# A fused four-layer kernel: evictions of first halves put ahead of weight conversions, three conversions put sooner, and the log-sum transposes put between two gate halves

## The reference

```python
q, k = rope(rms(aq)), rope(rms(ak))
ya = sliding_window_sink_attention(q, k, v, sink) * silu(ag)
qk = silu(causal_depthwise_conv(concat([mq, mk]), conv_w, conv_b))
hm = rms_norm(mlstm_chunkwise(*split(qk), mv, log_i, log_f))
ym = hm * sigmoid(mo) * silu(mgate)
x = x + concat([ya, ym]) @ w_out
```

## Time and the profile before

| what | value |
|---|---|
| median of 3 runs | 3051.35 us (3050.33 to 3055.56) |
| profiled execution: its own time | 3051.55 us |
| profiled execution: span in the trace | 3049.7 us |
| mean granted TensorE clock | 0.987 |
| PE busy | 2944.1 us, 97% |
| DVE, ACT, POOL busy | 53%, 41%, 6% |
| DMA | 250.24 MB, 82 GB/s on average |

### The profile page before, as it was taken

One profiled execution on the slowest core, in us unless ns is written; L12 is line 12 of the kernel. 1 busy time (PEld: TensorE's weight loads), 2 busy tenths in 40 slices (PEclk: granted clock), 3 DMA queues, 4 the chain that ended last, 5 costly groups with the idle time before them and its releaser, 6 DMA issues.

```text
span 3049.7 us, 44919 instructions
## 1 busy us (share of the span) xinstructions
PE 2944.1 (97%) x18366; PEld 2568.1 (84%) x18366; DVE 1629.9 (53%) x3259; ACT 1262.7 (41%) x2640; POOL 187.1 (6%) x207
## 2 busy tenths in 40 slices
PE   8999999999999999999999999999999999999998
PEld 7898888988888899898888877887888888877886
DVE  6767545367674453677433554325677433554334
ACT  5555423255553233566324433223566323433222
POOL 2100000020000000100000000000100000000000
PEclk9999999999999999999999999999999999999999
DMA  3111322211113222322232222233322232222322
GB/s 115 51 51 52 106 68 63 87 56 51 59 51 106 68 88 82 117 72 79 85 116 85 75 77 76 90 97 97 114 84 79 76 119 89 77 76 77 96 97 76
DMA packets 99735, 250.24 MB, mean 82 GB/s; under 512 B 8597, under 2 KB 44845, under 8 KB 99274
## 3 DMA queue, kind: packets, MB, share of 16 engines
q1 hardware_dynamic: 99530, 247.37, 25.8%
HBM read 239.60 MB, written 6.50 MB: 81 GB/s over the span
## 4 chain that ended last, share of the span: by engine, by line
PE 80%; DVE 11%; ACT 5%; issue 2%; POOL 1%; DMA 1%; DVEq 0%; SPq 0%; POOLq 0%; ACTq 0%
PE ps L92 77%; PE ps L95 3%; ACT Z L98 2%; DVE Z L109 2%; DVE Z L101 2%; DVE ZR L101 1%; DVE cl L101 1%; ACT ch L98 1%; DVE Z L105 1%; DVE stat L122 1%; DVE Z L119 1%; DMA st<-in_stream_dram 1%; POOL stat L101 1%; DVE stat L109 1%; ACT sq L98 1%
## 5 line engine op out<-in xcount | busy, mean ns | idle before, releaser
L101 DVE TENSOR_TENSOR cl<-st,ch 128x1024 fp32r<-128x1024 f32 (+1 forms) x436 | 500.4, 1156 | 635.2 <-ACT ch L98 634.8
L92 PE MATMUL ps<-hl,ch 128*128 128x264 f32 (+1 forms) x2816 | 835.7, 340 | 0.0
L92 PE MATMUL ps<-hh,ch 128*128 128x512 f32 (+1 forms) x2624 | 806.3, 347 | 26.6 <-ACT Z L98 12.3
L92 PE MATMUL ps<-hh,cl 128*128 128x512 f32 (+1 forms) x2624 | 795.3, 343 | 0.0
L98 ACT ACTIVATE ch<-st 128x1024 fp32r<-128x1024 f32 (+1 forms) x436 | 428.9, 990 | 513.5 <-PE ps L92 428.1
L92 PEld LDWEIGHTS ps<-hh,ch 128*128 128x128 f32 x2624 | 455.1, 191 | 98.1 <-ACT Z L98 18.4
L92 PEld LDWEIGHTS ps<-hl,ch 128*128 128x128 f32 x2816 | 487.2, 190 | 59.5
L92 PEld LDWEIGHTS ps<-hh,cl 128*128 128x128 f32 x2624 | 456.2, 190 | 59.2
L92 PE MATMUL ps<-ZR,ch 128*128 128x264 f32 (+2 forms) x1856 | 445.9, 337 | 5.5 <-DVE cl L101 5.1
L98 ACT ACTIVATE Z<-ps 64x128 f32<-64x128 f32 (+7 forms) x506 | 217.3, 437 | 432.1 <-PE ps L92 318.5
L92 PEld LDWEIGHTS ps<-ZR,ch 128*128 128x128 f32 x1856 | 305.3, 190 | 48.9 <-issue 12.8
(11 more groups left out here) (133 smaller groups left out, 3211.1 us busy)
## 6 DMA issues: line engine op xcount, KB each, us to landing
st<-in_stream_dram SPq DMA_DIRECT2D x372, 512.0 KB, 3.5
st<-in_stream_dram SPq DMA_DIRECT2D x64, 256.0 KB, 3.3
Z<-decay_rows SPq DMA_DIRECT2D x8, 904.0 KB, 6.1
Z<-bias_lines SPq DMA_DIRECT2D x16, 448.0 KB, 3.8
ya_spill<-Z SPq DMA_DIRECT2D x8, 512.0 KB, 4.6
Z<-ya_spill SPq DMA_DIRECT2D x2, 2048.0 KB, 7.5
Z<-in_x_dram SPq DMA_DIRECT2D x4, 512.0 KB, 5.3
Z<-in_mem_dram SPq DMA_DIRECT2D x2, 1024.0 KB, 5.7
```

Source lines behind the costliest of these rows:

```text
L92: return Ins(self, self.e and self.e.matmul(o, a, b, start=start, stop=stop, skip_group_check=True))
L101: return Ins(self, self.e and self.e.tensor_tensor(o, a, b, op))
```

## The change

It moves steps in the list, and adds or removes none.

1. `proj` of a first half no longer puts its conversion at once. The conversion is owed, and `put` places it right behind the next step whose name ends in `ev`. This concerns every first half that goes through `proj`, some 90 of them; `projr`, `mvmm`, `kvk`, `dvmm`, `lvmm` and the units with one half are as before.
2. In `mem_kv` the conversion that followed `kvk` 3 stands ahead of it ("one memory piece").
3. In `block1` the conversion that followed the first `o1` stands ahead of ys 6 to 13 ("one output piece").
4. In `block2` the first half of `lg(0)` stands between `mq(1)` and `lse2`, and its second half ahead of group 1's `pn`, where both stood.

```diff
+        self.owed = False
 
     def put(self, *step):
         self.o.append(step)
+        if self.owed and step[0].endswith("ev"):
+            self.owed = False
+            self.weights()
...
     def proj(self, key, nid, T, u, h, last=None):
         last = h == 1 if last is None else last
         self.put("proj", key, nid, T, u, h, last)
-        for _ in range(2 if last and not h else 1):
-            self.weights()
+        if last:
+            for _ in range(1 if h else 2):
+                self.weights()
+        else:
+            self.owed = True
...
         def step(c):
             if c < 4:
+                if c == 3:
+                    self.weights()
                 self.put("kvk", l, c, self.take(2, l, "kv", c))
-                self.weights()
+                if c < 3:
+                    self.weights()
                 return
...
+        self.weights()
         for k in range(6, 14):
             put("ys", l, k)
...
             if n != 1:
                 put("o1", l, n, p, 0, 8)
-                self.weights()
+                if n:
+                    self.weights()
...
-        def lg(c):
-            u = self.unit(2, l, 8704 + 256 * c)
-            for h in range(2):
+        def lg(c, hs=(0, 1)):
+            if 0 in hs:
+                st["lg"] = self.unit(2, l, 8704 + 256 * c)
+            u = st["lg"]
+            for h in hs:
                 self.proj(("lg", l, 2 * c + h), nid, 512, u, h)
                 put("lgev", l, 2 * c + h, self.nsq(), self.ngr())
         put("lse0", l)
         mq(0)
         put("lse1", l)
         mq(1)
+        lg(0, (0,))
         put("lse2", l)
         for g in range(3):
             if g == 1:
-                lg(0)
+                lg(0, (1,))
```

## The result

The changed kernel takes 3078.6 us, the median of 4 runs (3077.29 to 3078.76), beside 3050.84 us for the kernel before in the same session (3047.77 to 3055.56). The ratio is 1.0092, 95% interval 1.008 to 1.0104: slower by 0.9%. The forecast had the sign and the places right and the size too small: +17.3 against about +27.8, and the range ended at 3076.

What follows compares the result with a forecast made beforehand. TensorE, busy 2944.1 of 3049.7 us (97%), was taken as the bound. Terms -9.1 -1.2 +15.0 +6.6 +4 +2 = +17.3, added to 3051.55, gave 3068.8 us; range 3057 to 3076.

Steps and rivals of the forecast that it cites:

- lse: Block 2's log-sum part: edits 1 and 4 make pn end 7.5 us later, which reaches PE; +15.0 for two layers.
- the single gap of over 5 us: Sign of being right: a new PE gap of 5 us or more ahead of eT 2, which waits for pn.
- fB, +6.6 of gap: Block 2's fB 0 and fB 1: DVE's copies start 1.46 and 1.84 us later; +6.6 for both layers.
- Clock, +4 at fB and +2 at eT: Half clock after new PE gaps: 1.0 us each at four fB gaps and, for each layer, at eT.
- My case of half clock at all six gaps in full: Rival: 1.7 us at each new gap (+4.2) and lse at 9, about 3076 us; chance 0.15.
- Block 1, -9.1 and -1.2 for the gate: Block 1: gaps -5.7 and clock -3.4 from edits 1 and 3; attention gate's half-clock stretch, both layers, -1.2.
- the query halves: Block 1: eviction first lets PE start earlier; -0.95 and -0.96 at step 3, -1.2 at halves 5 and 7, -1.7 clock.
- mA 0: Block 1: a conversion comes beside another one on DVE; +0.8 us (0.3 to 1.3) in the first layer.
- The price of one stretch, 1.7: A half-clock stretch of 3.4 us costs about 1.7 us where PE is dense.
- Edit 2, 0: Memory piece: its cl waits for its copy either way, 0; without the cover of ACT's norms, 1.2 us per layer.
- little change: Rival: lse costs 3.8 a layer, no new half clock at fB or eT; +3.9, 3055.5 us; chance 0.10.
- faster: Rival: lateness at lse and fB does not reach PE; block 1's -10.3 is left, 3041.2 us; chance 0.04.

Runs made afterwards that it cites:

- experiment 4: The changed kernel, but first halves mg 2 and gt(0,0), ahead of fB 0 and fB 1, convert before their eviction as before: 3064.54 us, 1.0046.
- experiment 8: The changed kernel with 12 unused identity products added in PE's gaps at fB 0 and fB 1 of each block 2 layer: 3069.62 us, 1.006.
- experiment 1: The changed kernel with eviction-first kept for block 1's halves only, edit 4 undone, edits 2 and 3 kept: 3043.16 us, 0.9972.
- experiment 3: The changed kernel with edit 4 undone, lg(0) whole again ahead of group 1's pn: 3061.34 us, 1.0033.
- experiment 9: The kernel of experiment 1 without eviction-first for attention gate 6, and with yasp 5 to 7 moved behind fB 2: 3042.35 us, 0.9971.
- experiment 10: The kernel of experiment 1 without eviction-first for attention gate 6: 3044.41 us, 0.998.
- experiment 2: The kernel before with edit 4 alone, the first half of lg(0) ahead of lse2: 3062.6 us, 1.0039.

## Why the prediction was wrong: the price of the lower clock, and edit 1 in block 1

**lse, +15.0 of lateness.** Right: the gap of 5.3, `pn` starting 10 us and ending 7.3 us late, and that all of it reaches PE (7.4). In the second layer it is 8.6, 1.3 of them because `lg(0)` ran at 0.50 for twice as long. Which row waits first was not right, nor the single gap of over 5 us: I had `eT` 2; it was `eT` 1, for group 0's products, and 1.51, 1.21 and 0.19.

**fB, +6.6 of gap.** Right to 0.05 us at both places.

**Clock, +4 at fB and +2 at eT.** This is the step that failed. At fB it is 7.5 to 9.0 (experiments 4 and 8), behind `eT` 2.0 and 2.5, and 1.3 in the second layer's `lg(0)`: together some 13.5 to 15 for the 6 that I took. Three things are in it. I took 1.0 of 1.7 as a mean for each gap at fB, and both gaps of 2.7 in both layers brought a stretch, worth 1.6 to 1.7 each in the rows; the one behind fB 2 also grew from 3.4 to 6.8 in the first layer. Behind `eT` I priced one stretch of 3.4 us, at most 1.7, and the clock stayed at 0.50 for 10 us, with waits of 1.51, 1.21 and 0.19 (in the second layer 1.42, 1.28 and 0.77) ahead of it and in it. And I had no term for a longer stretch in `lg(0)`. My case of half clock at all six gaps in full was still 1.7 for each, so the range's upper end rested on the same prices.

**Trainium skill, "TensorE: Matmul & The Clock Gate", section "Why this matters for your kernels".** The Trainium skill says there that only idle gaps longer than those at fB bring the clock down, so by it the four stretches would have stayed away. The runs decide against it: in the traces with gaps of 2.71 at fB, 11 of 12 such gaps are followed by 0.50, and with matmuls in them, in experiment 8, the time falls by 9.0 us.

**Block 1, -9.1 and -1.2 for the gate.** Edit 3 was right (-5.2 measured, -4.6 forecast). Edit 1 was forecast at -2.8 net in gaps there and up to -2.9 in clock, and is worth nothing that can be measured alone (0.9995). This is the second step that failed. The reasoning "the eviction is 0.95 us earlier, so PE is" was used at the query halves without the check that I made at the convolution half, whether the scores behind it come earlier too. At mA 0 I had put +0.8 in the first layer and nothing in the second, and it came as about 0 and +1.56.

**The price of one stretch, 1.7.** The two rates that I gave for it, 0.194 and 0.114 us, make only 1.4 of 3.4 us. The 1.7 is nearer to what the rows show: PE falls back by 1.62 and 1.66 us in the stretches behind the second layer's two gaps at fB.

**Edit 2, 0,** was not tried by itself; it is in the kernels of experiments 1, 3, 9 and 10, none of which leaves room for more than a microsecond or two. At the memory piece itself the traces with it and without it differ by less than 1 us.

Sum of the corrections, from the traces: clock some +7.5 (2.0 and 2.5 behind `eT`, 1.3 in `lg(0)`, 7.7 at fB, for 6), block 1 some +2.6 (-7.7 for -10.3), which is +27.4 for +17.3, beside +26.8 between the two traces and +27.8 between the medians. The parts are each uncertain by a microsecond or more, so that they meet so closely is in part luck. The rivals: "little change" needed lse at 3.8 a layer and "faster" needed less than 4 of 27.6 us to reach PE; experiments 2 and 4 exclude both.

Open is when a gap of this size brings the lower clock and for how long: the second layer's `lg(0)` had 6.8 us of it and the first's 3.4 behind the same gap of 5.3. What sets that, no run here shows.

## What to carry to other kernels

A step's eviction goes ahead of a conversion only where someone waits for the eviction; where a later copy on the same engine is what PE waits for, the conversion belongs ahead of the eviction, in the time when the engine waits for PE anyway. When long serial work on one engine feeds two others, don't fill PE's wait with work whose eviction that engine must do first. And price a new wait of PE of 2.4 us or more, and several of 1.2 to 1.5 us close together, with the clock behind it, and not for one stretch alone where small waits follow; work that nobody reads, in the bank that is overwritten next, is a cheap test and here a cheap cure (0.9957 with it, 0.998 and 0.9984 without).

## What the hardware showed that I had not expected

In the same instructions the clock differs between executions. The kernel of experiment 2 has block 1 as the kernel before, and in this stretch after the attention gate's wait:

```profile
314.50:320.50 6.00, 6.00 (x51) 6.00 (x51) 4.38 (x13) 2.40 (x7) 0.00 (x0) 1.00 0.28 87
```

The kernel before had 27 matmuls there at 0.50:

```profile
314.50:320.50 6.00, 6.00 (x27) 6.00 (x28) 3.46 (x12) 1.62 (x6) 0.00 (x0) 0.50 0.28 87
```

At the end of block 1 the one is 5 us ahead of the other. A difference of some microseconds between two traces is therefore no evidence for a cause in block 1, and the forecast's clock gains there were read from such a single trace. Of the waits of 2.38 to 2.43 us at lse, 13 of 14 in all traces were followed by a stretch at 0.50 (not the first layer's in experiment 9), and of waits of 2.38 to 2.48 us in block 1 only 6 of 12. At fB it was 11 of 12 gaps of 2.71: in the trace of experiment 3 the first layer's fB 0 has a gap of 2.71 and none behind it.
